# A two-layer hybrid decoder step: the gram levels of its recurrence summed in another engine, and the mixer's order of work rewritten

## What is computed

```python
def hgrn2_chunked(q, logf, v, S0):          # chunks of 64 tokens
    ...
    def step(S, inp):
        qc, lfc, kc, vc = inp
        ...
        A = jnp.einsum('bhtk,bhsk,bhtsk->bhts', qc, kc, dec)
        o = jnp.einsum('bhts,bhsv->bhtv', A, vc) + jnp.einsum('bhtk,bhkv->bhtv', qc * jnp.exp(b), S)
        ...
def sink_attend(q, k, v, q_pos, k_pos, sinks):   # window 128, 8 query heads, 2 key heads
    ...
    m = jnp.maximum(jnp.max(s, axis=-1, keepdims=True), sink)
    p = jnp.exp(s - m)
    p = p / (jnp.sum(p, axis=-1, keepdims=True) + jnp.exp(sink - m))
    return jnp.einsum('bnhgqk,bnkhd->bnqhgd', p.astype(v.dtype), v)
def mixer(h, pos0, kv_prev, S0, conv_prev, lb, w_in, w_out, sinks, gnorm, cw):
    z = h @ w_in
    qa, ka, va, qh, fh, ih, gh, bc, cc, hc = jnp.split(z, np.cumsum(sizes)[:-1].tolist(), axis=-1)
    ...
    o_hg = rms_norm(o_hg, gnorm).reshape(B, T, D_HG).astype(h.dtype) * jax.nn.silu(gh)
    y_conv = bc * y_conv
    out = jnp.concatenate([o_attn, o_hg, y_conv], axis=-1) @ w_out
    return out, new_k, new_v, S_new, conv_new
```

## Time and profile before

| | |
|---|---|
| median of 3 runs | 1426.69 us (1426.34 to 1428.79) |
| the profiled execution: its time, its span | 1424.1 us, 1422.3 us |
| mean granted TensorE clock | 0.976 |
| TensorE busy | 1342.7 us, 94% |
| VectorE busy | 689.1 us, 48% |
| ScalarE busy | 558.2 us, 39% |
| GpSimd busy | 86.5 us, 6% |
| DMA | 255.49 MB, mean 180 GB/s |

### The profile page before, as it was taken

One profiled execution on the slowest core, in us unless ns is written; L12 is line 12 of the kernel. 1 busy time (PEld: TensorE's weight loads), 2 busy tenths in 40 slices (PEclk: granted clock), 3 DMA queues, 4 the chain that ended last, 5 costly groups with the idle time before them and its releaser, 6 DMA issues.

```text
span 1422.3 us, 23388 instructions
## 1 busy us (share of the span) xinstructions
PE 1342.7 (94%) x10190; PEld 1258.3 (88%) x10190; DVE 689.1 (48%) x715; ACT 558.2 (39%) x703; POOL 86.5 (6%) x93
## 2 busy tenths in 40 slices
PE   4999999999979899999999999999997889999997
PEld 2899999979857699999979999997996679999996
DVE  0534434357773634444354444435688554444433
ACT  2532333354433543333344333424451455333331
POOL 0000000000530000000000000000025100000000
PEclk9999999999988999999999999999998899999998
DMA  9655656474534734446473444746545132444440
GB/s 366 246 208 195 215 202 235 165 277 148 183 144 177 288 119 148 148 159 252 152 296 113 143 156 148 264 153 250 182 168 218 49 108 97 151 148 147 168 158 37
DMA packets 50376, 255.49 MB, mean 180 GB/s; under 512 B 7022, under 2 KB 12014, under 8 KB 30062
## 3 DMA queue, kind: packets, MB, share of 16 engines
q1 hardware_dynamic: 50110, 253.08, 49.3%
q0 software_dynamic: 176, 1.09, 0.2%
HBM read 249.26 MB, written 4.89 MB: 179 GB/s over the span
## 4 chain that ended last, share of the span: by engine, by line
PE 84%; ACT 5%; DVE 4%; DMA 2%; POOL 2%; issue 2%; SPq 0%; DVEq 0%; ACTq 0%; POOLq 0%
PE PS L484 26%; PE PS L486 25%; PE PS L485 25%; PE PS L493 2%; PE PS L540 2%; ACT hmh L944 1%; ACT sq L944 1%; DMA raw<-in_w_in 1%; DVE raw L1403 1%; POOL y L1673 1%; DVE sq L1407 1%; POOL z L1666 1%; DMA stage<-in_ada_w 1%; DMA x<-in_x 1%; PE PS L731 0%
## 5 line engine op out<-in xcount | busy, mean ns | idle before, releaser
L484 PE MATMUL PS<-hmh,WHI 128*128 128x320 f32 x1856 | 579.7, 312 | 11.5 <-DVE hml L1236 10.4
L485 PE MATMUL PS<-hml,WHI 128*128 128x320 f32 x1856 | 573.3, 309 | 0.0
L486 PE MATMUL PS<-hmh,WLO 128*128 128x320 f32 x1856 | 573.3, 309 | 0.0
L1174 DVE TENSOR_TENSOR WLO<-raw,WHI 128x2048 fp32r<-128x2048 f32 (+1 forms) x148 | 366.2, 2474 | 394.6 <-ACT WHI L908 394.6
L908 ACT ACTIVATE WHI<-raw 128x2048 fp32r<-128x2048 f32 (+1 forms) x148 | 303.7, 2052 | 349.0 <-PE PS L486 346.0
L484 PEld LDWEIGHTS PS<-hmh,WHI 128*128 128x128 f32 x1856 | 350.0, 189 | 24.7 <-issue 12.8
L485 PEld LDWEIGHTS PS<-hml,WHI 128*128 128x128 f32 x1856 | 350.2, 189 | 0.2
L486 PEld LDWEIGHTS PS<-hmh,WLO 128*128 128x128 f32 x1856 | 349.8, 188 | 0.0
L484 PE MATMUL PS<-hhl,WHI 128*128 128x320 f32 x704 | 216.8, 308 | 0.0
L486 PE MATMUL PS<-hhl,WLO 128*128 128x320 f32 x704 | 216.7, 308 | 0.0
L485 PE MATMUL PS<-hhl,WHI 128*128 128x320 f32 x704 | 216.7, 308 | 0.0
(11 more groups left out here) (227 smaller groups left out, 873.6 us busy)
## 6 DMA issues: line engine op xcount, KB each, us to landing
raw<-in_w_in SPq DMA_DIRECT2D x88, 1024.0 KB, 4.8
raw<-in_w_out SPq DMA_DIRECT2D x32, 1408.0 KB, 6.0
stage<-in_ada_w SPq DMA_DIRECT2D x76, 512.0 KB, 7.6
ada<-in_ada_w SPq DMA_DIRECT2D x52, 512.0 KB, 7.0
raw<-in_m_in SPq DMA_DIRECT2D x20, 1024.0 KB, 4.8
raw<-in_m_out SPq DMA_DIRECT2D x8, 1024.0 KB, 6.2
z<-in_ada_w SPq DMA_DIRECT2D x4, 1024.0 KB, 11.6
big<-in_ada_w SPq DMA_DIRECT2D x2, 1024.0 KB, 16.1
```

The costliest lines, as they stand in the source:

```text
L484: mm(out, hi, rhi, start=first, stop=False)
L485: mm(out, hi, rlo, start=False, stop=False)
L486: return mm(out, lo, rhi, start=False, stop=last)
L1174: tt(WLO[:, slot, 0:width], raw[:, slot, 0:width], WHI[:, slot, 0:width].bitcast(F32), ALU.subtract).then_inc(s_lo[slot], 1)
```

## The change

In words, and then the core of the diff.

1. *Levels.* The reductions L1407 and the buffer `AT` go. `am` becomes two buffers, and TensorE's `levels(n)` multiplies the values with each masked level (n = group), all accumulating in banks 4 and 5; with them 128 products per layer instead of 20. State times query is added to the same banks afterwards (six products).
2. *Scores between the groups.* Sample scores (one unit per key head) and the second block's prompt scores (four units) go through one bank, 6, in six `unit(u)`; each unit waits until VectorE has emptied the bank (`un`). `SC1` and `SS` now lie in the tails of the split weights' buffers, one per key head. The state increments move behind the fifth group, into banks 2 and 3; the first block's scores behind the sixth.
3. *Samples first.* Exponentials run in the order samples, second block (two halves), first block. The samples' transposes follow right behind the last partial, their values ahead of the prompt's; 24 of the output projection's matmuls (k = 4 to 7 of slot 0) move into the mixer, ahead of the prompt's values.
4. *Slot 1 of the output weights.* Its low split (VectorE) moves to the mixer's end; the load of slot 1 of the weights 1 (SP), which waits for it, moves behind the six pieces. `MIX_GAP` has three places now (ada, M, N), and two chunks use bank 7 instead of 6.
5. *GpSimd.* Rotation first, then two copies that were VectorE's (L1455, L1456), then q times exp b, the convolution, and `vm`, which lies in `big` now and waits for the sixth gram group.

```diff
-MIX_GAP = ["ada", "M"] * 3
+MIX_GAP = ["ada", "M", "N"] * 2
...
-BANKS = [6, 7, 6, 7, 6, 4, 6, 7, 6, 7, 6, 4, 6, 7, 4, 6, 7, 6]
+BANKS = [6, 7, 6, 7, 6, 4, 6, 7, 7, 7, 6, 4, 6, 7, 4, 6, 7, 7]
...
-STAGE = {"S0": (0, 1024), "S1": (2048, 3072), "M": (0, 2560),
+STAGE = {"S0": (0, 1024), "S1": (2048, 3072), "M": (0, 2560), "N": (1024, 3584),
...
-        am = tail[:, :, 0:NL * CH]
-        it_, kt_, at_ = (sf[:, n * 768:(n + 1) * 768] for n in range(3))
...
+        am = [tail[:, :, 0:NL * CH], sf[:, 1536:1536 + 2 * NL * CH].rearrange("p (e k) -> p e k", e=2)]
...
-        vm = yf[0:64, 0:2048].rearrange("p (h b v) -> p h b v", h=4, b=NB)
+        vm = big[0:64, 1032:3080].rearrange("p (h b v) -> p h b v", h=4, b=NB)
         SC0 = big[:, 0:8 * 129].rearrange("p (h k) -> p h k", h=8)
...
+        wt = [split[:, 2 * n:2 * n + 2, W_IN:W_OUT] for n in (0, 1)]
+        SC1 = [w[:, :, 0:514].rearrange("p s (t k) -> p s t k", t=2) for w in wt]
+        SS = [w[:, :, 514:707] for w in wt]
```

SP:

```diff
-                def out_weights(it):
-                    for slot in (0, 1):
-                        weights(l * ITS + OFF_MO + it, slot, MOUT[l * 2 * IT_MO + it * 2 + slot], W_IN)
-                out_weights(0)
+                def out_weights(it, slot):
+                    weights(l * ITS + OFF_MO + it, slot, MOUT[l * 2 * IT_MO + it * 2 + slot], W_IN)
+                out_weights(0, 0)
+                out_weights(0, 1)
                 piece(AT_MIX[l])
                 sp.wait_ge(s_used[1], l * ITS + OFF_MI + IT_MI + 1)
                 for p in range(AT_MIX[l] + 1, AT_MIX[l] + 6):
                     piece(p)
                     if p == AT_MIX[l] + 3:
-                        out_weights(1)
+                        out_weights(1, 0)
+                out_weights(1, 1)
```

TensorE, the new functions and their order (the old loop of the groups, goes):

```diff
+                def levels(n):
+                    a, cp = groups[n]
+                    pe.wait_ge(ev["am"], 12 * l + 2 * n + 2)
+                    hold(pe)
+                    top = NL if cp < 2 else NLS
+                    for i in range(top):
+                        for c in members(cp):
+                            bank, col = place(a, c)
+                            rows = slice(64 * (c % 2), 64 * (c % 2) + 64)
+                            for e in (0, 1):
+                                last = mm(PS[64 * e:64 * e + 64, bank, col:col + CH],
+                                          vtok[rows, c // 2, a * P + 64 * e:a * P + 64 * e + 64],
+                                          am[n % 2][rows, e, i * CH:(i + 1) * CH], start=(n == 0 and i == 0),
+                                          stop=(i == top - 1), skip_group_check=True)
+                    last.then_inc(ev["lv"], 1)
...
+                def unit(u):
+                    if u:
+                        pe.wait_ge(ev["un"], 6 * l + u)
...
+                            mm(PS[p0:p0 + 32, 6, c0:c0 + WIN], q, kc[rows, b, 0:WIN], start=True, stop=True)
+                            last = mm(PS[p0:p0 + 32, 6, c0 + WIN:c0 + 192], q, kc[rows, :, WIN:WIN + TS],
+                                      start=True, stop=True)
+                    else:
+                        n, s = (u - 2) // 2, (u - 2) % 2
+                        rows = slice(64 * n, 64 * n + 64)
+                        for t in (0, 1):
+                            last = mm(PS[:, 6, t * 256:(t + 1) * 256], z[rows, Z_A + 2 * s + t, P:TP],
+                                      z[rows, Z_K, 0:TP], start=True, stop=True)
+                    last.then_inc(ev["us"], 1)
...
+                grams(0)
+                grams(1)
+                pe.wait_ge(s_mod, done + 1)
+                pe.wait_ge(ev["rp"], 3 * l + 3)
+                pe.wait_ge(ev["qk"], l + 1)
...
+                unit(0)
+                pe.wait_ge(ev["kt"], l + 1)
+                for n in range(6):
+                    if n < 4:
+                        grams(n + 2)
+                    levels(n)
+                    if n == 0:
+                        partial(p + 1)
+                    if n == 1:
+                        turned(done)
+                    if n in (2, 3):
+                        partial(p + n)
+                    if n == 4:
...
+                        for c2 in (0, 1):
...
+                        last.then_inc(ev["ds"], 1)
+                    if n < 5:
+                        unit(n + 1)
```

```diff
+                pe.wait_ge(ev["ptd"], 4 * l + 2)
+                pe.wait_ge(ev["mixl"], 4 * l + 2)
+                hold(pe)
+                for t in (0, 1):
+                    for k in range(4, KT):
+                        mm3(PS[:, t, 0:T], 0, k * 256 + t * P, hmh[:, k, :], hml[:, k, :], k == 4, False)
+                pe.wait_ge(ev["mixl"], 4 * l + 3)
...
-                        pe.wait_ge(ev["mixl"], 4 * l + 3)
-                        for ks in (range(4, KT), range(4)):
-                            if ks[0] == 0:
-                                pe.wait_ge(ev["mixl"], 4 * (l + 1))
```

VectorE:

```diff
+                def masked(n):
+                    rows, w = (slice(0, P), NL) if n % 3 < 2 else (slice(0, 64), NLS)
+                    dve.wait_ge(ev["gr"], 6 * l + n + 1)
+                    if n >= 2:
+                        dve.wait_ge(ev["lv"], 6 * l + n - 1)
+                    for e in (0, 1):
+                        tt(am[n % 2][rows, e, 0:w * CH], PS[rows, 2 - 2 * (n % 2) + e, 0:w * CH], gram[rows, 0:w * CH],
+                           ALU.mult).then_inc(ev["am"], 1)
...
+                    dve.wait_ge(ev["us"], 6 * l + u + 1)
+                    if u < 2:
...
+                    else:
+                        n, s = (u - 2) // 2, (u - 2) % 2
+                        stt(SC1[n][:, s, :, 0:256], PS[:, 6, :].rearrange("p (t k) -> p t k", t=2), SCALE,
+                            mskp.unsqueeze(1).to_broadcast([P, 2, 256]), ALU.mult, ALU.add).then_inc(ev["un"], 1)
...
+                masked(0)
+                masked(1)
+                unit(0)
+                masked(2)
+                unit(1)
+                dve.wait_ge(ev["un"], 6 * l + 2)
...
+                masked(3)
                 mod_out(chunk_of(3 * l + 1, 2))
+                unit(2)
+                masked(4)
+                unit(3)
+                masked(5)
+                top(0)
+                unit(4)
...
+                lo_split(1, l * ITS + OFF_MO, W_IN)
...
-                    lo_split(1, g + 1, W_IN)
+                    if it < IT_MI - 1:
+                        lo_split(1, g + 1, W_IN)
```

GpSimd:

```diff
-                        pool.wait_ge(ev["dec"], l + 1)
-                        tt(eb, eb, z[:, Z_Q:Z_Q + 2, :].rearrange("p a t -> p (a t)"), ALU.mult)\
-                            .then_inc(ev["ebq"], 1)
+                pool.wait_ge(ev["rp"], 3 * l + 3)
+                g_.tensor_copy(kc[:, :, WIN:WIN + TS], z[:, Z_K, TP:T].rearrange("p (b t) -> p b t", t=TS))
+                g_.tensor_copy(qs.rearrange("p b (a t) -> p a b t", t=TS),
+                               z[:, Z_A:Z_A + 4, TP:T].rearrange("p k (b t) -> p k b t", t=TS)).then_inc(ev["qk"], 1)
+                pool.wait_ge(ev["dec"], l + 1)
+                tt(eb, eb, z[:, Z_Q:Z_Q + 2, :].rearrange("p a t -> p (a t)"), ALU.mult).then_inc(ev["ebq"], 1)
                 conv(l)
...
-                pool.wait_ge(ev["obk"], l + 1)
+                pool.wait_ge(ev["gr"], 6 * (l + 1))
```

402 lines of the change are left out of this document (179 added, 223 removed).

## The result

| | before | changed |
|---|---|---|
| median, lowest to highest | 1426.51 us (1425.24 to 1428.79) | 1440.36 us (1437.31 to 1441.99) |
| profiled execution: time, span, mean clock | 1424.1, 1422.3 us, 0.976 | 1441.99, 1440.2 us, 0.969 |
| TensorE, VectorE busy | 1342.7, 689.1 us | 1352.3, 676.6 us |

The ratio of the times is 1.0073, with a 95% interval of 1.0048 to 1.0099: slower by 0.7%, where 0.8% faster was forecast. Repeated on another chip the ratio was 1.0064 (1.0041 to 1.0087).

A forecast was written before the change was run, and what follows sets the result against it. VectorE bounds the mixer first, TensorE after the change; the low half completes at 437.4 instead of 443.8. Gains of 7.1 (layer 1) and 4.4 us (layer 0) sum to 11.5: 1412.6, plus 2.6 for the median, 1415; range 1403 to 1424.

The forecast's parts named there:

- Start: Mixer's beginning: last rotation needs 0.8 us instead of 2.79, so VectorE starts its masks about 385.2, not 387.5.
- The level product at 0.033: Price of one level product on TensorE, taken as a gram product's 0.033 us; the possible range was up to 0.13.
- rival D: Single score bank 6: six hand-overs between TensorE and VectorE stall 1 us each, no gain remains: 1427; chance 0.08.
- TensorE is now the bound ... Together 27.5: 409.5.: Layer 0 mixer from 382.0: TensorE's work sums to 27.5 us, so state products end at 409.5 instead of 414.3.
- The middle of the softmax: After the state products: VectorE and ScalarE finish the softmax, so TensorE can transpose the sample weights at 414.7.
- The tail, 19.2, and 3.5 for the low clock: TensorE from 414.7 to the last low half: 19.2 us, plus 3.5 for 7 us at low clock: 437.4.
- Behind the mixer, layer 1: Projection after layer 1's mixer ends 25.2 us behind the low half instead of 27.5; layer 1 gains 7.1.
- Layer 0 and the queue: Next weights land 30.7 us behind the low half, not 25.3; 2.0 us lost, so layer 0 gains 4.4.
- B: Mixer's front: scores, levels and values at the low clock, or level products at 0.13; near 1442 or 1440; chance 0.08.
- Rival A: Mixer: TensorE stays at 2.4 GHz, returning the 3.5 us twice: 1408; chance 0.25.
- a microsecond or two more: Layer 0's DMA queue: extra gain beyond rival A, given as the source of the range's lower end, 1403.

The follow-up runs named there:

- r_slot1_late: Changed kernel with level sums back on VectorE, slot 1 of the output weights split and loaded as before, ada_w pieces 2 to 5 loaded and multiplied late: 1432.6 us.
- b_dup: Kernel before the change with each gram product issued twice: ratio 1.0136 to the kernel before (1448.3 us).
- b_wide: Kernel before the change with one added product of 448 columns ahead of each gram group: ratio 1.0008 to the kernel before.
- b_dup_quiet: Kernel before, gram products issued twice, mixers' six ada_w pieces loading 64 of 1024 columns, output weights 1 loaded after the last mask: ratio 1.0006.

## Why the prediction was wrong

The sum said 1415 for 1440.4, outside the range.

- *Start.* Right: masks at 385.03 (385.2 predicted), the last rotation 0.87 us instead of 2.79 (0.8 predicted).
- *The level product at 0.033.* Right while TensorE has code: 53 of its instructions, two a product, took 0.99 us, 0.037 a product. The hand-overs of bank 6 (rival D) showed no long waits: VectorE was the one that waited.
- *"TensorE is now the bound ... Together 27.5: 409.5."* This is the step that failed. The state products ended at 426.5, 17.0 later. The waits for issue are 0.55 + 4.84 + 3.62 = 9.0 of it, and the low clock 16.6/2 = 8.3: together 17.3. The sum added durations of products as if their instructions were always there; it had no term for code that comes late. Its rows could hardly have warned of it. L699's "[3.37 <-issue]" looks like such a wait and is one for VectorE's masks, as the prediction had it (VectorE the bound, TensorE idle from 398). The only late code in the mixers before is the 0.84 us shown above. VectorE's pace, 2.76 us a group, spread TensorE's small products out; packets started 4.1, 7.5 and 9.4 us apart from 386 on and came in time, although the DMA engines were as busy. The change took that pace away and put two packets more into each mixer.
- *The middle of the softmax.* Right in length: 4.6 us from the end of L784 to L795 (5.2 predicted).
- *The tail, 19.2, and 3.5 for the low clock.* 21.2 in all from L795 to the last low half, with the clock at 0.50 up to 436; 1.5 us less than the 22.7 predicted.
- *Behind the mixer, layer 1.* Right: L549 follows the low half by 25.1 us (25.2 predicted; before 27.4).
- *Layer 0 and the queue.* Right in kind: the weights land 29.5 us after the low half (30.7), ScalarE waits 9.90 us for them (about 10), L549 follows at 34.4 (34.2). Two small errors cancel in that: the weights came 1.2 us sooner, and L549 4.9 us behind them instead of 3.5. L543 starts at 43.8 instead of 41.7: after its 9.18 us of idle TensorE ran at 0.50 until 490.7, which is in no term.
- *The rivals.* B had the size (1442) and a part of the mechanism, the low clock over some 17 us of work. But it had no cause for it, and half of the loss in that front is TensorE standing still. Rival A, for which the prediction named the Trainium skill ("TensorE: Matmul & The Clock Gate", "Part 1: The HAM clock gate": sustained activity lifts the clock), did not come: the order was denser on paper, and the stalls broke it. The trace agrees as far as the clock fell inside the idle of 4.84 us (0.65 in the microsecond from 388, 0.50 from 389) and inside that of 3.62 us (0.50 from 402). It disagrees in r_slot1_late, where the clock is low from 390 to past 426 with TensorE busy in most of that time.
- *The range.* Its lower end, 1403, doesn't follow from the text: A is 1408, and "a microsecond or two more" gives 1406. It changes nothing here.

By the batches, the sums on TensorE cost some 17 us (1.0064 against 0.9948), and the other parts together gain about 7 (0.9948 against 1).

## What to carry to other kernels

Count instructions as well as microseconds wherever products are small: here a packet of some 216 instructions lasts 16 us of big products and 2 us of 64x64 ones, and it is fetched by DMA beside the loads. When TensorE idles on "issue", first look at where. In front of a run of products it can be a plain wait for another engine: look for work of that engine which ended 0.1 us or so before. Inside a run, with a packet of q8 landing just before its end, it is late code. That is not slack to be filled: it grows with the instructions added there and with the loads beside them. A cheap test is the pair of b_dup and b_wide: the same engine time once in many instructions and once in few, put where it should be hidden.

## What the runs showed that was not expected

- TensorE's code came in packets of 16 KB, each itself 0.9 to 1.7 us long. With hardly a load beside them they cost TensorE 0.4 to 1.3 us (b_dup_quiet), with loads mostly 2 to 5.5, and TensorE resumed 1.2 to 1.6 us after a packet had landed.
- The extra packets alone were harmless in the kernel before: 128 more products a layer changed the time by 0.06% (0.9981 to 1.0031) without loads and by 1.36% with them.
- The same word "issue" stood for two things: late code, and a wait for VectorE's masks whose end the profile did not put down to VectorE (L699, 3.37 us in each layer).
- In r_slot1_late TensorE kept the low clock for over 30 us in which it was busy 3.63 of 6 us first and then 5.44 to 6.00 of every 6.
